# Splitting each weight tile with one instruction of 2048 columns on ACT and on DVE

## Chip, cores and metric

The kernel runs on one core of a Trainium2 chip. The metric is the device time of one execution in microseconds, as the median of several runs.

## What is computed

Two transformer blocks, one behind the other, on 256 tokens of width 2048, in float32. Cut to what matters:

```python
# first block
x = layer_norm(ALPHA * x + hybrid_mixer(x))           # sparse latent attention + block attention, gated, out1
x = layer_norm(ALPHA * x + mem_cross_attention(x, mem))
x = layer_norm(ALPHA * x + (silu(x @ w_g) * (x @ w_u)) @ w_down)        # up1, down1
# second block; shift, scale, gate = silu(c) @ w_ada + b_ada
x = x + gate1 * (concat(fourier_mix(u), mlstm_bidirectional(q, k, v, gates)) @ w_out)   # out2
x = x + gate2 * ((silu(conv(a)) * conv(v)) @ w_down)                    # up2, down2
return rms_norm(x)
```

Nearly all of the work is products of the 256 tokens with weight matrices of the first and the second block, 438 tiles of 1 MB.

## The kernel before

**Stream of weights.** The weights lie in memory as one stream of tiles, each 128 partitions by 2048 float32 columns (1 MB), in the order in which the stages use them (`TILES`, line 62): latent, q_idx, v_moba, w_uk, w_uv, qk, gate_a, gates, out1, the four of the memory attention, up1 (88 tiles), down1 (44), the mLSTM's, fourier, out2, up2 (88), down2 (44). SyncE loads tile g into `raw[g % 4]` (lines 388 to 396) once `lo_ready` tells that tile g − 4 has been split.

**Split.** TensorE multiplies in the type fp32r. For float32 accuracy every operand is split in a high part (rounded) and a low part (the rest), and each product is three: high by high, high by low, low by high. For a weight tile, ScalarE (ACT) makes the high part, `whi <- raw`, in `upper(g)` (line 499, the instruction is line 514), and VectorE (DVE) makes the low part, `wlo = raw - whi`, in `rest(g)` (line 920, instruction line 929). Both work by halves of 1024 columns. `whi` and `wlo` have four slots of 1024 columns each, two tiles' worth. ACT may overwrite a slot once TensorE (PE) has counted up `weights_used` for the half four before:

```python
if h >= 4:
    act.wait_ge(weights_used, at(h - 3, i, 2 * per))
```

DVE waits for `hi_ready` of the half, PE for `lo_ready` of the half. `at(n, i, per)` is the semaphore value n in the first round of a hardware loop and per more in each further one.

**Products.** `product` (line 1533) takes one half of a tile: in T form (line 1559) 24 matmuls of 256 columns, in N form (line 1563) of up to 512. In up1, up2 and most projections four tiles fill a chunk, a pair of PSUM banks, which ACT or DVE reads out when PE is through with it. `wide_tile` (line 1575) serves out1, o_mem, down1, out2 and down2: 24 matmuls of 512 columns a tile (line 1600) into all eight banks; it also waits for `slo_ready`, the low part of the activations, which DVE makes tile by tile (lines 1120, 1136) from the high part of ACT (line 686).

**Order of the work.** Every engine runs its own program, written out by hand. In up1, ACT runs eight calls of `upper` a loop turn, and behind the one with s = 3 it reads a finished chunk:

```python
if s == 3:
    act.wait_ge(weights_used, at(through(g0 + s), i, 16))
    act.wait_ge(pair_read[(c0 + 1) % 2], at(reads(c0 - 1), i, 1))
    act.activation(silu[:], pair(c0), ACT.Silu).then_inc(pair_read[c0 % 2], 1)
```

Before a Silu, a Sigmoid or an Exp the compiler puts an ACT_TABLE_LOAD, and another at the head of a loop for the copies behind it. DVE does, beside the splits, `modulation` (line 961), 96 steps of the product silu(c) @ w_ada on tiles of 2048 columns that GpSimd's queue loads: 8 in out1, 66 in up1, 22 in down1. In the turns of a wide stage (`later_turns`) DVE's order is, for s = 0 to 3, low part of the activations (line 1136), `rest`, and for s = 1 and 2 a `modulation`. The row sums of the normalizations (lines 1173 to 1225), the split of the memory activations (`mhi` line 718, `mlo` line 1232) and the read-outs (line 553 and others) stand between the calls at the ends of the stages.

Of the kernel before, what the change touches and what calls it, by code (L numbers as in the profile page):

```python
# [6 lines left out]
F32 = mybir.dt.float32  # L7
# [3 lines left out]
ALU = mybir.AluOpType  # L11
ACT = mybir.ActivationFunctionType
# [106 lines left out]
def at(first, i=None, per=0):  # L119

    return first if i is None else i * per + first


def two_blocks(nc, x, xt, memt, stream, w_ada, cols, rows, ln_g, ln_b, norm_f, c_row, gate_bias, dft, out, max_store, gate_store):
    with ExitStack() as ctx:  # L125
        def sem(name):
            return ctx.enter_context(nc.semaphore(name))
# [3 lines left out]
        def sb(name, shape, dt=F32, offset=None):  # L131

            here = place[0] if offset is None else offset
            if offset is None:
                size = int(np.prod(shape[1:])) * (2 if dt == BF16 else 4)
                place[0] += -(-size // 32) * 32
            return nc.alloc_sbuf_tensor_at(name, shape, dt, offset=here)


        raw = [sb(f"raw{s}", [P, D]) for s in range(4)]  # L140
        whi = sb("whi", [P, 4, 1024], F32R)
        wlo = sb("wlo", [P, 4, 1024], F32R)
# [127 lines left out]
        first_half_landed = sem("first_half_landed")  # L270
        raw_landed = [sem(f"raw_landed{s}") for s in range(4)]
        hi_ready = sem("hi_ready")
        lo_ready = sem("lo_ready")
        weights_used = sem("weights_used")
# [216 lines left out]
        def _(act):  # L491
# [10 lines left out]
            def upper(g, i=None, per=0):  # L502

                if g >= G:
                    return
                for half in range(2):
                    h = 2 * g + half
                    if g == 0 and half == 0:
                        act.wait_ge(first_half_landed, 16)
                    elif g == 0 or half == 0:  # L510
                        act.wait_ge(raw_landed[g % 4], at(16 * (g // 4 + 1), i, 4 * per))
                    if h >= 4:
                        act.wait_ge(weights_used, at(h - 3, i, 2 * per))
                    act.activation(whi[:, h % 4], raw[g % 4][:, 1024 * half:1024 * half + 1024], ACT.Copy)\  # L514
                       .then_inc(hi_ready, 1)

            def x_first_upper(b):

# [46 lines left out]
            for b in range(2):  # L565
                x_first_upper(b)
            upper(g0)
            for b in range(2, 4):
                x_first_upper(b)
            upper(g0 + 1)  # L570
            for b in range(4, 8):
                x_first_upper(b)
            upper(g0 + 2)
            upper(g0 + 3)
            act.wait_ge(pair_read[CH["latent"] % 2], reads(CH["latent"]))
# [17 lines left out]
            for n in range(8):  # L593
                g = AT["v_moba"] + n
# [10 lines left out]
            g = AT["w_uk"]  # L605
# [3 lines left out]
            g = AT["w_uv"]  # L609
# [4 lines left out]
            with act.Fori(0, 3) as i:  # L614
                for s in range(8):
                    upper(g0 + s + 1, i, 8)
                    if s % 4 == 3:
                        read_out(CH["qk"] + s // 4, g0 + s, qk[:, bass.ds(at(s - 3, i, 8), 4)].rearrange("p k t -> p (k t)"),
                                 i=i, per=8)
# [3 lines left out]
            with act.Fori(0, 2) as i:  # L623
                for q in range(4):
                    g = g0 + 2 * q
# [32 lines left out]
            with act.Fori(0, 2) as i:  # L658
                for unit in range(2):
                    g, c = g0 + 8 * unit, c0 + 3 * unit  # L660
# [258 lines left out]
        def _(dve):  # L919
            order = Order(dve, dve_order)  # L920

            def rest(g, i=None, per=0):

                if g >= G:
                    return
                for half in range(2):
                    h = 2 * g + half
                    dve.wait_ge(hi_ready, at(h + 1, i, 2 * per))
                    dve.tensor_tensor(wlo[:, h % 4], raw[g % 4][:, 1024 * half:1024 * half + 1024], whi[:, h % 4].bitcast(F32),  # L929
                                      ALU.subtract).then_inc(lo_ready, 1)  # L930

            def x_first_rest(b):

# [31 lines left out]
            for b in range(2):  # L965
                x_first_rest(b)
            rest(g0)
            for b in range(2, 4):
                x_first_rest(b)
            rest(g0 + 1)  # L970
            for b in range(4, 8):
                x_first_rest(b)
            rest(g0 + 2)
            rest(g0 + 3)
            dve.wait_ge(weights_used, through(g0 + 2))
# [104 lines left out]
            with dve.Fori(0, 2) as i:  # L1080
                order.enter(i, 24)
                for q in range(4):
                    g = g0 + 2 * q
# [64 lines left out]
            for unit in range(4):  # L1148
                g, c = AT["gates"] + 8 * unit, CH["gates"] + 3 * unit
# [268 lines left out]
            for n in range(4):  # L1418
                g = AT["lstm_o"] + 4 * n
# [569 lines left out]
```

## Time and profile before

| | before |
|---|---|
| median of 3 runs | 2600.51 us (2598.02 to 2602.15) |
| profiled execution, its own time | 2601.53 us |
| its span | 2599.9 us |
| granted TensorE clock, mean | 0.985 |
| busy: PE, DVE, ACT | 97%, 63%, 48% |
| DMA | 582.19 MB, mean 224 GB/s |
| chain that ended last, largest items | PE L1559 18%, PE L1600 12% |

The busy shares are sums over the whole span. Idle time in the groups of the profile is the time that an engine stood before an instruction, with what ended it ("<-"). In a timeline a row is one or several instructions in a row of the same kind: start, time, engine, line, and in brackets the idle time before and who ended it. Engine times of neighbouring instructions overlap by some hundredths of a microsecond.

### The profile page before, as it was taken

The numbers are of one execution on the slowest core, as the hardware profiler recorded it, in microseconds if no ns is written. First come the engines' busy times: TensorE is split into PE (matmuls) and PEld (weight loads), VectorE is DVE, ScalarE is ACT, GpSimd is POOL, SyncE is SP. The second block draws the span as 40 slices with busy tenths as digits, with TensorE's granted clock in tenths as the row PEclk, the third lists the DMA queues.
The fourth block names the chain that finished last, engine by engine and source line by source line (L and its number), as shares of the span: only waits on it lengthen the run. The fifth ranks groups of instructions, "written<-read, shape, count | busy, mean of one in ns | idle before, by whom it ended". The sixth has DMA issues, their size and how long they took to land. (4 is left out here: it accounts for less than half of the span.)

```text
span 2599.9 us, 45820 instructions
## 1 busy us (share of the span) xinstructions
PE 2511.7 (97%) x17960; PEld 2346.5 (90%) x17960; DVE 1641.5 (63%) x1908; ACT 1247.5 (48%) x1503; POOL 88.8 (3%) x143
## 2 busy tenths in 40 slices
PE   7999999999989999999999969999899999999997
PEld 7799999998979999999888868978799999998885
DVE  5564675457767777777777764555666666665555
ACT  4444564444544445454444454444555555554443
POOL 0000000000100000000000000000000000000000
PEclk9999999999999999999999989999899999999998
DMA  7455445569548898989877725435455555555552
GB/s 268 166 185 192 153 146 182 189 252 361 201 156 326 333 351 325 350 325 349 345 289 289 268 99 205 173 120 192 148 194 194 193 192 191 192 199 180 192 193 97
DMA packets 80968, 582.19 MB, mean 224 GB/s; under 512 B 9052, under 2 KB 9212, under 8 KB 10752
## 3 DMA queue, kind: packets, MB, share of 16 engines
q1 hardware_dynamic: 64224, 462.97, 48.5%
q0 software_dynamic: 14528, 104.63, 10.5%
q10 hardware_dynamic: 2144, 13.58, 1.4%
q8 instruction: 52, 0.85, 0.1%
q14 instruction: 20, 0.16, 0.0%
HBM read 579.02 MB, written 2.12 MB: 224 GB/s over the span
## 5 line engine op out<-in xcount | busy, mean ns | idle before, releaser
L929 DVE TENSOR_TENSOR wlo<-raw,whi 128x1024 fp32r<-128x1024 f32 x876 | 1056.9, 1223 | 753.4 <-ACT whi L514 750.0
L514 ACT ACTIVATE whi<-raw 128x1024 fp32r<-128x1024 f32 x876 | 918.3, 1061 | 1007.6 <-PE ps L1559 591.8
L1559 PE MATMUL ps<-xhi,whi 128*128 128x256 f32 x4176 | 1156.1, 277 | 10.7 <-DVE xlo L953 4.5
L1559 PE MATMUL ps<-xhi,wlo 128*128 128x256 f32 x4176 | 1151.6, 276 | 0.0
L1559 PE MATMUL ps<-xlo,whi 128*128 128x256 f32 x4176 | 1151.6, 276 | 0.0
L1559 PEld LDWEIGHTS ps<-xhi,whi 128*128 128x128 f32 x4176 | 786.5, 188 | 12.0 <-DVE xlo L953 4.3
L1559 PEld LDWEIGHTS ps<-xlo,whi 128*128 128x128 f32 x4176 | 786.6, 188 | 0.3
L1559 PEld LDWEIGHTS ps<-xhi,wlo 128*128 128x128 f32 x4176 | 786.2, 188 | 0.0
L961 DVE SCALAR_TENSOR_TENSOR ada<-ada,cb 128x2048 f32<-128x2048 f32 x96 | 219.4, 2286 | 11.3 <-DMA ada<-in_w_ada 11.1
L1600 PE MATMUL ps<-whi,dhi 128*128 128x512 f32 x704 | 217.7, 391 | 4.1 <-DVE conv L1470 4.1
L1600 PE MATMUL ps<-wlo,dhi 128*128 128x512 f32 x704 | 217.6, 390 | 0.0
L1600 PE MATMUL ps<-whi,dlo 128*128 128x512 f32 x704 | 217.6, 390 | 0.0
L1600 PEld LDWEIGHTS ps<-whi,dhi 128*128 128x128 f32 x704 | 132.5, 189 | 31.9 <-issue 4.5
L1600 PEld LDWEIGHTS ps<-whi,dlo 128*128 128x128 f32 x704 | 132.7, 188 | 27.8
L1600 PEld LDWEIGHTS ps<-wlo,dhi 128*128 128x128 f32 x704 | 132.7, 188 | 27.7
L1563 PE MATMUL ps<-whi,xhi 128*128 128x512 f32 (+1 forms) x224 | 88.4, 395 | 11.1 <-DVE wlo L929 10.2
L1600 PE MATMUL ps<-whi,shi 128*128 128x512 f32 x288 | 89.7, 393 | 2.9 <-DVE slo L1120 2.9
L1600 PE MATMUL ps<-whi,slo 128*128 128x512 f32 x288 | 89.3, 391 | 0.0
L1600 PE MATMUL ps<-wlo,shi 128*128 128x512 f32 x288 | 89.2, 391 | 0.0
L1563 PE MATMUL ps<-whi,xlo 128*128 128x512 f32 (+1 forms) x224 | 86.5, 386 | 0.0
L1563 PE MATMUL ps<-wlo,xhi 128*128 128x512 f32 (+1 forms) x224 | 86.4, 386 | 0.0
L1470 DVE SCALAR_TENSOR_TENSOR conv<-ps,col,conv 128x255 f32<-128x255 f32 x176 | 72.7, 475 | 18.5 <-ACT conv L880 18.5
(272 smaller groups left out, 1852.8 us busy)
## 6 DMA issues: line engine op xcount, KB each, us to landing
raw<-in_stream SPq DMA_DIRECT2D x437, 1024.0 KB, 4.8
ada<-in_w_ada POOLq DMA_DIRECT2D x96, 1024.0 KB, 6.4
gamma<-in_ln_g ACTq DMA_DIRECT2D x3, 1024.0 KB, 9.8
beta<-in_ln_b ACTq DMA_DIRECT2D x3, 1024.0 KB, 14.4
xT<-in_xt SPq DMA_DIRECT2D x4, 512.0 KB, 11.2
mem_part<-in_memt ACTq DMA_DIRECT2D x2, 1024.0 KB, 6.7
res<-in_x ACTq DMA_DIRECT2D x1, 2048.0 KB, 14.1
gate_row<-gate_store POOLq DMA_DIRECT2D x2, 1024.0 KB, 5.3
```

Of the source, the lines that this page charges most:

```text
L514: act.activation(whi[:, h % 4], raw[g % 4][:, 1024 * half:1024 * half + 1024], ACT.Copy)\
L929: dve.tensor_tensor(wlo[:, h % 4], raw[g % 4][:, 1024 * half:1024 * half + 1024], whi[:, h % 4].bitcast(F32), ALU.subtract).then_inc(lo_re ...
L961: dve.scalar_tensor_tensor(out=ada[slot][:], in0=ada[slot][:], scalar=1.0, in1=cb[:], op0=ALU.mult, op1=ALU.mult, accum_out=mod[:, bass.ds ...
L1470: ins = dve.scalar_tensor_tensor(out=conv[:, q, S * m + to:S * m + to + S - 1], in0=bank[:, S * m + fro:S * m + fro + S - 1], scalar=col[: ...
L1559: ins = pe.matmul(o, w[:, k, P * m:P * m + P], a(kt), start=begins and n == 0 and m % 2 == 0, stop=ends and n == 2, skip_group_check=True)
L1563: ins = pe.matmul(o, a(kt)[:, P * m:P * m + P], w[:, k, :], start=begins and n == 0, stop=ends and n == 2, skip_group_check=True)
L1600: ins = pe.matmul(ps[:, 4 * t + 2 * half + n], a[:, s, P * t:P * t + P], w[:, h % 4, 512 * n:512 * n + 512], start=first and a is hi and w ...
```

## The change

From tile 2 on, `upper` issues one ACT instruction over the whole tile and `rest` one DVE instruction. ACT waits until PE has counted up `weights_used` for both halves of tile g − 2 (2g − 2), DVE for `hi_ready` of both halves, and each adds 2 to its semaphore. Tiles 0 and 1 are split by halves as before. PE's program, SyncE's, the buffers and every other step are unchanged.

```diff
--- before.py
+++ after.py
@@ -503,16 +503,18 @@
 
                 if g >= G:
                     return
-                for half in range(2):
-                    h = 2 * g + half
-                    if g == 0 and half == 0:
-                        act.wait_ge(first_half_landed, 16)
-                    elif g == 0 or half == 0:
-                        act.wait_ge(raw_landed[g % 4], at(16 * (g // 4 + 1), i, 4 * per))
-                    if h >= 4:
-                        act.wait_ge(weights_used, at(h - 3, i, 2 * per))
-                    act.activation(whi[:, h % 4], raw[g % 4][:, 1024 * half:1024 * half + 1024], ACT.Copy)\
-                       .then_inc(hi_ready, 1)
+                if g < 2:
+                    for half in range(2):
+                        if g == 0 and half == 0:
+                            act.wait_ge(first_half_landed, 16)
+                        else:
+                            act.wait_ge(raw_landed[g], 16)
+                        act.activation(whi[:, 2 * g + half], raw[g][:, 1024 * half:1024 * half + 1024], ACT.Copy).then_inc(hi_ready, 1)
+                    return
+                act.wait_ge(raw_landed[g % 4], at(16 * (g // 4 + 1), i, 4 * per))
+                act.wait_ge(weights_used, at(2 * g - 2, i, 2 * per))
+                act.activation(whi[:, 2 * (g % 2):2 * (g % 2) + 2].rearrange("p h n -> p (h n)"), raw[g % 4][:], ACT.Copy)\
+                   .then_inc(hi_ready, 2)
 
             def x_first_upper(b):
 
@@ -923,11 +925,17 @@
 
                 if g >= G:
                     return
-                for half in range(2):
-                    h = 2 * g + half
-                    dve.wait_ge(hi_ready, at(h + 1, i, 2 * per))
-                    dve.tensor_tensor(wlo[:, h % 4], raw[g % 4][:, 1024 * half:1024 * half + 1024], whi[:, h % 4].bitcast(F32),
-                                      ALU.subtract).then_inc(lo_ready, 1)
+                if g < 2:
+                    for half in range(2):
+                        h = 2 * g + half
+                        dve.wait_ge(hi_ready, h + 1)
+                        dve.tensor_tensor(wlo[:, h], raw[g][:, 1024 * half:1024 * half + 1024], whi[:, h].bitcast(F32),
+                                          ALU.subtract).then_inc(lo_ready, 1)
+                    return
+                dve.wait_ge(hi_ready, at(2 * g + 2, i, 2 * per))
+                both = slice(2 * (g % 2), 2 * (g % 2) + 2)
+                dve.tensor_tensor(wlo[:, both].rearrange("p h n -> p (h n)"), raw[g % 4][:],
+                                  whi[:, both].rearrange("p h n -> p (h n)").bitcast(F32), ALU.subtract).then_inc(lo_ready, 2)
 
             def x_first_rest(b):
```

In the program after, lines of ACT behind this place stand 2 further down and those of DVE 8.

The change moves the first wait of a loop turn relative to the table load. ACT, head of the loop of up1, before (L514 is the split, ISA and REGISTER_ALU set and count the values waited for, L779 is the silu read-out):

```order
L773 ISA
L513 ISA [waits raw_landed2]
L514 ACT_TABLE_LOAD
L514 ACTIVATE whi<-raw_51 128x1024 [waits weights_used]
L513 REGISTER_ALU
L514 ACTIVATE whi<-raw_51 128x1024 [waits weights_used]
```

and after (L516 is the split):

```order
L775 ISA
L515 ISA [waits raw_landed2]
L516 ACT_TABLE_LOAD [waits weights_used]
L516 ACTIVATE whi<-raw_51 128x2048
L515 REGISTER_ALU [waits raw_landed3]
L516 ACTIVATE whi<-raw_52 128x2048 [waits weights_used]
```

The table load came before the wait for `weights_used`; now it carries that wait. The same pair of rows stands at the head of the loop of up2.

ACT around the silu read-out of up1, before:

```order
L513 REGISTER_ALU
L514 ACTIVATE whi<-raw_50 128x1024 [waits weights_used]
L777 REGISTER_ALU
L778 REGISTER_ALU [waits weights_used]
L779 ACT_TABLE_LOAD
L779 ACTIVATE silu<-ps 128x1024 [waits pair_read1]
L513 REGISTER_ALU [waits raw_landed2]
L514 ACTIVATE whi<-raw_51 128x1024 [waits weights_used] x2
L513 REGISTER_ALU [waits raw_landed3]
L514 ACTIVATE whi<-raw_52 128x1024 [waits weights_used]
```

and after:

```order
L516 ACTIVATE whi<-raw_50 128x2048 [waits weights_used]
L779 REGISTER_ALU
L780 REGISTER_ALU [waits weights_used]
L781 ACT_TABLE_LOAD
L781 ACTIVATE silu<-ps 128x1024 [waits pair_read1]
L516 ACTIVATE whi<-raw_51 128x2048 [waits weights_used,raw_landed2]
L515 REGISTER_ALU [waits raw_landed3]
L516 ACTIVATE whi<-raw_52 128x2048 [waits weights_used]
```

The read-out has kept its place between two tiles; behind it come two splits of a half before and one of a whole tile after.

DVE in a later turn of down1, tiles 2 and 3 of the turn, before (L1136 the low part of the activations, L929 the split, L961 `modulation`):

```order
L1136 TENSOR_TENSOR dlo_118<-hid,dhi 128x256
L928 REGISTER_ALU
L929 TENSOR_TENSOR wlo<-raw_52,whi 128x1024 [waits hi_ready]
L928 REGISTER_ALU
L929 TENSOR_TENSOR wlo<-raw_52,whi 128x1024 [waits hi_ready]
L960 ISA
L961 ISA [waits ada_landed0]
L961 SCALAR_TENSOR_TENSOR ada_98,mod<-ada_98,cb 128x2048
L1135 REGISTER_ALU
L1136 ISA [waits shi_ready]
L1136 TENSOR_TENSOR dlo_118<-hid,dhi 128x256
```

and after (lines 8 further down, the split L937):

```order
L1144 TENSOR_TENSOR dlo_118<-hid,dhi 128x256
L935 REGISTER_ALU
L937 TENSOR_TENSOR wlo<-raw_52,whi 128x2048 [waits hi_ready]
L968 ISA
L969 ISA [waits ada_landed0]
L969 SCALAR_TENSOR_TENSOR ada_98,mod<-ada_98,cb 128x2048
L1143 REGISTER_ALU
L1144 ISA [waits shi_ready]
L1144 TENSOR_TENSOR dlo_118<-hid,dhi 128x256
```

The modulation still stands between the split and the low part of the next tile's activations; the split ahead of it is one instruction of twice the width.

## Rows read from the trace of the kernel before

**Rows 1.** The page, sections 1 and 5 (busy us, mean ns, idle, releaser)

```profile
PE 2511.7 (97%) x17960; PEld 2346.5 (90%) x17960; DVE 1641.5 (63%) x1908; ACT 1247.5 (48%) x1503; POOL 88.8 (3%) x143
...
L929 DVE TENSOR_TENSOR wlo<-raw,whi 128x1024 fp32r<-128x1024 f32 x876 | 1056.9, 1223 | 753.4 <-ACT whi L514 750.0
L514 ACT ACTIVATE whi<-raw 128x1024 fp32r<-128x1024 f32 x876 | 918.3, 1061 | 1007.6 <-PE ps L1559 591.8
L1559 PE MATMUL ps<-xhi,whi 128*128 128x256 f32 x4176 | 1156.1, 277 | 10.7 <-DVE xlo L953 4.5
```

**Rows 2.** Windows: stretch, length, busy us, clock, DMA share (up1, down1, up2, down2)

```profile
780.00:1258.00 478.00, 478.00 (x4210) 477.62 (x4209) 364.66 (x325) 225.02 (x215) 34.90 (x66) 1.00 0.88 336
1262.00:1480.00 218.00, 218.00 (x963) 180.50 (x963) 153.26 (x158) 96.95 (x119) 10.56 (x20) 1.00 0.78 300
1862.00:2330.00 468.00, 468.00 (x4132) 468.00 (x4131) 287.06 (x351) 255.04 (x288) 0.00 (x0) 1.00 0.55 195
2345.00:2575.00 230.00, 230.00 (x1015) 190.41 (x1015) 115.41 (x124) 100.31 (x123) 0.00 (x0) 1.00 0.50 178
```

**Rows 3.** Waits of PE for the split: us, times, longest

```profile
PE ps L1563 <- DVE wlo L929: 10.2, 1, 10.2
...
PE ps L1559 <- DVE wlo L929: 2.9, 1, 2.9
```

**Rows 4.** Timeline in up2, one half on ACT and DVE

```profile
1899.29 1.06 ACT L514 ACTIVATE whi<-raw 128x1024 fp32r<-128x1024 f32 x1 [1.66 <-PE ps L1559]
...
1900.39 1.23 DVE L929 TENSOR_TENSOR wlo<-raw,whi 128x1024 fp32r<-128x1024 f32 x1 [1.49 <-ACT whi L514]
```

**Rows 5.** Groups by shape on ACT and DVE, the rows of 2048 columns

```profile
L701 ACT ACTIVATE ps<-res 128x2048 f32<-128x2048 f32 x6 | 11.3, 1881 | 29.4 <-DVE res L1225 22.9 <-DVE res L1193 6.5
L592 ACT ACTIVATE cb<-cb 128x2048 f32<-128x2048 f32 x1 | 1.9, 1922 | 0.0
...
L1225 DVE TENSOR_TENSOR res<-res,xn 128x2048 f32<-128x2048 f32 x4 | 9.2, 2292 | 0.1
```

**Rows 6.** Timeline at the start, the tile that PE waited for

```profile
45.63 3.90 ACT L514 ACTIVATE whi<-raw 128x1024 fp32r<-128x1024 f32 x4
46.72 4.63 DVE L929 TENSOR_TENSOR wlo<-raw,whi 128x1024 fp32r<-128x1024 f32 x4 [0.53 <-ACT whi L514]
...
48.00 0.58 PE L1559 MATMUL ps<-xhi,whi 128*128 128x256 f32 x1 [2.94 <-DVE wlo L929]
```

**Rows 7.** Timeline of DVE in down1, a modulation and the low part

```profile
1329.08 2.28 DVE L961 SCALAR_TENSOR_TENSOR ada<-ada,cb 128x2048 f32<-128x2048 f32 x1
...
1331.30 0.42 DVE L1136 TENSOR_TENSOR dlo<-hid,dhi 128x256 fp32r<-128x256 f32 x1
```

**Rows 8.** Timeline of ACT in up1, silu read-out and loop head

```profile
886.24 1.28 ACT L779 ACT_TABLE_LOAD   x1 [4.44 <-PE ps L1559]
...
888.46 2.94 ACT L514 ACTIVATE whi<-raw 128x1024 fp32r<-128x1024 f32 x3
...
903.59 1.28 ACT L514 ACT_TABLE_LOAD   x1
905.22 1.06 ACT L514 ACTIVATE whi<-raw 128x1024 fp32r<-128x1024 f32 x1 [0.35 <-PE ps L1559]
```

**Rows 9.** Timeline of ACT at a gate's read-out and at that of lq

```profile
470.80 1.57 ACT L654 ACTIVATE sig<-ps,col 128x256 f32<-128x256 f32 x4 [4.61 <-PE ps L1559]
...
1550.92 1.03 ACT L553 ACTIVATE lq<-ps 128x1024 f32<-128x1024 f32 x1 [4.38 <-PE ps L1559]
...
1553.81 3.89 ACT L514 ACTIVATE whi<-raw 128x1024 fp32r<-128x1024 f32 x4
```

**Rows 10.** Timeline at the memory split on DVE and the entry of up1

```profile
654.81 2.35 DVE L1232 TENSOR_TENSOR mlo<-mem_part,mhi 128x1024 fp32r<-128x1024 f32 x2
...
780.09 3.91 ACT L514 ACTIVATE whi<-raw 128x1024 fp32r<-128x1024 f32 x4
...
782.50 0.35 PE L1559 MATMUL ps<-xhi,whi 128*128 128x256 f32 x1
```

## Prediction

> **What bounds the kernel now.** I read the page first. PE is busy for 2511.7 us of the span, 97% of it, and DVE for 63% and ACT for 48%; the split of the weights is by far the largest item of both, 876 instructions of 1223 ns on DVE and 876 of 1061 ns on ACT [rows 1]. The last columns of these two rows matter as much: before its splits DVE stood idle for 753.4 us in all, waiting for ACT, and ACT for 1007.6 us, waiting for PE. So neither engine is short of time on average; ACT waits for slots that PE gives back. Then the windows by stage: in up1, down1, up2 and down2 the busy time of PE equals the window to the last digit [rows 2], so no stall hides there and every stall that the change makes in them is new time. Then the waits of PE: for `wlo` it waited twice in the whole program, 10.2 and 2.9 us, both in the first 50 us [rows 3]. The bound is PE, and the question is only whether the split of a tile still arrives in time.
>
> **What the change does to the slack.** Measure everything from the start S of a tile on PE. In the timeline an ACT split of a half runs 1.06 us after 1.66 us of waiting for PE, so a half comes every 2.72 us and a tile lasts 5.44 [rows 4]; its 48 matmuls then stand 0.113 us apart, while one lasts 277 ns [rows 1], so the last one of a tile ends about 0.17 us into the next tile. With the step of a semaphore behind it, a release comes about 0.2 us after S. A half needs 1.06 us on ACT and 1.22 us on DVE, with 0.04 us from one to the other (1899.29 plus 1.06, then 1900.39) [rows 4].
>
> Before, a half could be split as soon as the half two tiles earlier was read, and only one half had to be ready when its tile began: from release to need lay three halves, 8.16 us, for a chain of 2.4 us, some 5.8 us of slack. After, a tile is split when the whole tile two before it is read, which is 0.2 us after the start of the tile in between, and must be whole before its own first matmul at 5.44: 5.24 us. The new chain is one ACT copy of 2048 columns, one DVE subtraction of 2048 columns, and two hand-overs. Neither instruction is in this trace. Bounds for ACT: from above twice 1061, 2122 ns [rows 1]; from below 1881 ns, the nearest row of the same width being 1922 ns (`cb`, SBUF to SBUF) [rows 5]; I take 1.92. For DVE: from above twice 1223, 2446 ns; the row of the same kind and width, a TENSOR_TENSOR of 2048 columns from SBUF to SBUF, says 2292 [rows 5], and from below nothing excludes a few per cent less, say 2.2; I take 2.29. The hand-over to PE is 0.06 us: a half begun at 46.72 ends at 47.94 and PE starts at 48.00 [rows 6]; I take 0.07. Sum: 1.92 + 0.04 + 2.29 + 0.07 = 4.32 us, against 5.24. **A plain tile keeps 0.92 us of slack**, and costs nothing. What covers it is that both engines are free at the release. Any ACT or DVE work that stands in the chain after the release costs its own length less 0.92.
>
> The DVE rows here hold a gain too: 2446 ns of two become 2290 of one, 0.16 us a tile, 68 us of DVE's busy time over 438 tiles, and 0.2 us a tile on ACT. I cost it at nothing where the engine is idle anyway (753 and 1008 us of idle time stand before the splits). The Trainium skill, in "VectorE: DVE Perf Modes", section "The TRN2 errata — SBUF-src ops pay a fixed extra latency per instruction", says that one large tile pays that latency once and many small ones each time. By that rule alone the kernel would gain, or stay; that result is the first rival. Another rule of the skill speaks against the change ("Perfetto Trace Analysis", section "Optimizing Scalar/DVE Operations"): where ACT and DVE are not saturated but hold up other engines, breaking instructions up may let work finish sooner. The change does the reverse.
>
> **The places where work stands in the chain.**
> - *down1 and out1: `modulation` ahead of the low part.* On DVE the order is: split, `modulation` (L961), low part of the activations (L1136), next split; PE needs that low part for its next tile. Before, 1329.08 to 1331.30 for the modulation, 2.22 us, and the low part at once behind it [rows 7], hidden. After, the split ends later: 0.2 + 1.96 (ACT and hand-over) + 2.22 (DVE to the next start) + 2.22 + 0.42 + 0.07 = 7.09 after S, against 5.44: 1.65 us of stall. The turn's second modulation starts from the tile so delayed and finishes 0.1 us before PE has run that tile, so nothing. Ten later turns of down1: 16.5 us. Three of out1: 5.0. There the split of the memory activations (`mlo`, 2.35 us) stands in the same position once: 1.7.
> - *up1: the silu read-out.* ACT reads a finished chunk when PE is through with it, ahead of the split that the same moment releases: table load 1.28 and silu, from 886.24 to 888.46, so 2.22 us [rows 8]. 2.22 − 0.92 = 1.30, 11 turns: 14.3 us. The 66 modulations of up1 come behind the split and ahead of the next release's DVE turn: 4.25 + 2.22 after the release, and DVE's next split cannot begin before 5.44 + 1.96. Hidden. The transfers are those of before; up1 uses 0.88 of the DMA engines [rows 2], and a refill has four tiles' time.
> - *Loop heads of up1 and up2: a table load that now waits.* Before, the load of 1.28 us ran at 903.59, ahead of the wait, and was done 0.35 us early [rows 8]. In the order of after the table load itself carries the wait for `weights_used`, because the copy's first wait moved in front of it. So 1.28 + 0.02 lies in the chain: 0.38 us each. Ten turns of either loop not counting the first: 7.6 us.
> - *mLSTM.* After the `lq` read-out ACT does a table load and an exponential: 1550.92 to 1553.81, 2.89 us [rows 9], less 0.92: 1.97; `lk` the same; the `g_m` one and a plain read of N form some 1.5 together. 5.4 us.
> - *Gates.* Four sigmoid read-outs of 1.57 us [rows 9], of which the next instruction overlaps 0.13 (as 1.03 and 1.28 us of silu and load take 2.22 and not 2.31 [rows 8]): 0.52 each, and one table load ahead of a read: 3.4. Some eight plain read-outs of 0.98 us: 0.06 each, 0.5.
> - *Start.* The split of the tile that PE waited for at 48.00 now must be whole: 45.63 + 4.32 = 49.95, so 1.95 later [rows 6]; two like it in the latent tiles, 0.6 each, between nothing and 1.95: 3.2 in all.
> - *Stage changes.* k_mem: the split of its first tile ends 1.9 us later, and `mlo` at 654.81 [rows 10] with the row sums behind it; its second tile 0.9 more; q_mem 0.5: 3.3. Entry of up1: ACT begins at 780.09 [rows 10]; the tile is whole at 784.41, and PE began it at 782.50 [rows 10]: 1.9. Entry of up2, in the same way, 1.4. Together 6.6.
> - *up2, out2, down2:* no modulation there; the taps and the silu come behind the split. Nothing beyond the loop heads.
>
> Sum: 23.2 (wide stages) + 14.3 + 7.6 + 5.4 + 3.9 + 3.2 + 6.6 = 64.2 us. The profiled execution took 2601.53 us; 2601.5 + 64.2 = 2665.7. The median of the three runs is 1.0 us lower, so **2664.7 us**, 2.5% slower. Bounds: with ACT at 2.12 and DVE at 2.45 the slack falls to 0.56, and the 65 or so stalls cost 0.36 more each, 20 us; with ACT at 1.88 and the loads of the loop heads uncounted it is 10 us less, and if half of the small terms (start, stage changes, gates) are absorbed another 6.
>
> **Rivals.** A measurement of this kernel can tell about 0.2% (5.2 us) from no change.
> - *Faster: fewer instructions win.* Where both engines stand in PE's way, at the six hand-overs between stages, some two splits each lie in front of row work: 12 × 0.16 to 0.2 us, and 13.1 us of PE's waits for `wlo` as their ceiling. −3 us: about 2597.5. It decides if the slack of a whole tile were above 2.9 us, so that neither silu nor modulation reached PE; the chain of 4.32 us against 5.24 speaks against it. 0.02.
> - *No change: the buffers hide it.* Same condition, without a gain: 2600. The idle 753 and 1008 us speak for it as totals; they are spread over the tiles and, with whole-tile slots, cannot be saved up for a crowded turn. That the change doesn't do what it says would end here too; the order of after shows the wide instructions from tile 2 on. 0.03.
> - *The table loads do not wait.* If the load runs ahead of the semaphore as now, 7.6 us fall away: 2657. 0.15.
> - *Every tile stalls.* If the chain of a plain tile were over 5.24 us, some 380 plain tiles pay the excess: 0.1 us each is 38 us, and the crowded turns pay 0.92 more each, 60 us: 2760 and above. It needs 0.92 us that no row shows; rows 5 speak against it. 0.05.
> - *The forecast*, stalls in crowded turns alone: 0.75.
>
> Range: 2644 to 2686, the forecast's own bounds and the third rival; the rest, one in ten, lies outside. Faster 0.02, same 0.03, slower 0.95.
>
> **What would show it.** In the profile of after: ACT 436 wide splits near 1.92 us, DVE near 2.29. PE less than full in up1 and down1, full in down2 and in plain tiles. Waits of PE: for `wlo` about 11 times 1.3 us and 10 times 0.4 in up1, ten of 0.4 in up2; for `dlo` ten times 1.65 us in down1. Wrong would be: PE waits in plain tiles; a chain from release to ready tile much off 4.3 us; down1 stalls twice a turn, or not at all; table loads at the loop heads that end before the release.

## Result: 2690.1 us, 3.4% slower

| | before | after |
|---|---|---|
| median of 3 runs | 2600.51 us | 2690.12 us (2689.82 to 2690.15) |
| span of the profiled execution | 2599.9 us | 2688.5 us |
| granted TensorE clock, mean | 0.985 | 0.983 |

The ratio after to before is 1.0344, 95% interval 1.033 to 1.0358: 89.6 us more, where 64 were forecast. The time lies 4 us above the range.

The page of after; the rows answer to [rows 1]:

```profile
PE 2536.3 (94%) x17960; PEld 2354.3 (88%) x17960; DVE 1597.0 (59%) x1472; ACT 1172.3 (44%) x1067; POOL 91.5 (3%) x143
...
L937 DVE TENSOR_TENSOR wlo<-raw,whi 128x2048 fp32r<-128x2048 f32 x436 | 999.4, 2292 | 970.0 <-ACT whi L516 969.9
L516 ACT ACTIVATE whi<-raw 128x2048 fp32r<-128x2048 f32 x436 | 836.2, 1918 | 1128.6 <-PE ps L1567 641.0
L1567 PE MATMUL ps<-xhi,whi 128*128 128x256 f32 x4176 | 1162.4, 278 | 39.5 <-DVE wlo L937 31.6
```

The two instructions took what the forecast took for them, 2292 and 1918 ns (2.29 and 1.92 us). DVE and ACT are less busy than before, 59 and 44% against 63 and 48%, and idle longer ahead of the split, 970 and 1129 us. The kernel became slower while both engines got less to do. PE's own busy time rose by 24.6 us, which the forecast did not have: the first matmuls behind each stall come more slowly, and at a few stage changes the granted clock is lower (both below).

The windows of up1, down1, up2 and down2, as [rows 2]:

```profile
804.00:1305.00 501.00, 482.48 (x4184) 478.16 (x4183) 357.21 (x230) 207.35 (x124) 35.02 (x66) 1.00 0.84 318
1320.00:1550.00 230.00, 214.22 (x928) 174.35 (x927) 143.95 (x115) 84.30 (x77) 10.09 (x20) 0.99 0.72 268
1950.00:2419.00 469.00, 465.90 (x4087) 463.94 (x4086) 271.97 (x263) 239.31 (x201) 0.00 (x0) 1.00 0.53 189
2440.00:2664.00 224.00, 224.00 (x990) 185.55 (x989) 107.40 (x81) 90.66 (x81) 0.00 (x0) 1.00 0.49 178
```

PE is short of the window by 18.5 us in up1, 15.8 in down1 and 3.1 in up2; in down2, where DVE has no modulation, it is full. The waits of PE, as [rows 3] (us in all, times, longest):

```profile
PE ps L1567 <- DVE wlo L937: 33.6, 43, 4.9
PE ps L1532 <- DVE xn L1216: 27.2, 2, 16.9
PE ps L1608 <- DVE dlo L1144: 17.5, 10, 1.9
...
PE ps L1532 <- DVE res L1201: 9.5, 2, 9.1
PE ps L1608 <- DVE slo L1144: 6.7, 4, 1.7
...
PE ps L1571 <- DVE wlo L937: 2.2, 2, 1.6
```

In before the two waits for row work, `xn` and `res`, were 4.0 us shorter together:

```profile
PE ps L1524 <- DVE xn L1208: 24.4, 2, 15.6
...
PE ps L1524 <- DVE res L1193: 8.3, 2, 7.9
```

Nearly all stalls sit where the forecast put them. Laid side by side matmul by matmul (start times of the n-th matmul in either trace), the two traces show that PE falls behind in steps, and between the steps it loses nothing: 1.55 us in each of the 11 silu turns of up1, 0.62 at each loop head of up1 and 0.61 at those of up2, 2.02 in a later turn of down1, 1.95 in four places of out1, 0.72 at each of four gates, 0.27 at the plain read-outs of qk. The forecast had no term for three of the steps: 1.26, 1.26 and 1.49 us at the ends of the memory attention, down1 and out2. There DVE's row work stands behind a split, now one of 2048 columns that ends later; at the end of the memory attention that split runs from 781.27 to 783.56 and the row work starts at 783.48 without a gap, while in before DVE had stood idle for 0.40 us, waiting for PE. By stage, in us:

| stage | forecast | measured |
|---|---|---|
| start to gates | 7.1 | 9.1 |
| attention, out1 | 6.7 | 8.6 |
| memory | 3.3 | 6.0 |
| up1 | 20.0 | 27.0 |
| down1 | 16.5 | 22.0 |
| mLSTM, out2 | 5.4 | 8.2 |
| up2 | 5.2 | 7.6 |
| down2 | 0 | 0.1 |
| sum | 64.2 | 88.6 |

**One silu turn, step by step.** Timeline of after in up1, ACT, then DVE and PE:

```profile
917.93 1.28 ACT L781 ACT_TABLE_LOAD   x1 [3.51 <-PE ps L1567]
919.22 1.03 ACT L781 ACTIVATE silu<-ps 128x1024 f32<-128x1024 f32 x1
920.15 1.91 ACT L516 ACTIVATE whi<-raw 128x2048 fp32r<-128x2048 f32 x1
```

```profile
922.16 2.29 DVE L937 TENSOR_TENSOR wlo<-raw,whi 128x2048 fp32r<-128x2048 f32 x1 [5.35 <-ACT whi L516]
...
924.51 0.39 PE L1567 MATMUL ps<-xhi,whi 128*128 128x256 f32 x1 [1.24 <-DVE wlo L937]
924.73 0.28 PE L1567 MATMUL ps<-xlo,whi 128*128 128x256 f32 x1
924.85 0.28 PE L1567 MATMUL ps<-xhi,wlo 128*128 128x256 f32 x1
```

PE began the tile in between at 917.67 (48 matmuls of 0.113 us before its last). ACT starts at 917.93, 0.26 us later, not 0.20. Silu moves the split by 2.22 us, as forecast. From the end of the split, 920.15 + 1.91 = 922.06, DVE needs 0.10 us to start, not 0.04. It ends at 924.45, and PE starts 0.06 later. That is 6.84 us after 917.67, so PE is 1.40 us late (a tile lasts 5.44); its first matmul then lasts 0.39 us and the second starts 0.22 behind it in place of 0.11, another 0.11, and the ten behind them lose 0.04 more. Together 1.55, against 1.30.

**The loop head** of up1, ACT in after:

```profile
941.23 1.28 ACT L516 ACT_TABLE_LOAD   x1 [3.50 <-PE ps L1567]
942.52 1.93 ACT L516 ACTIVATE whi<-raw 128x2048 fp32r<-128x2048 f32 x1
```

ACT stands idle for 3.50 us until PE releases the slot, and only then runs the table load; in before the load was over by then [rows 8].

**A turn of down1**, DVE, then PE:

```profile
1385.51 2.29 DVE L937 TENSOR_TENSOR wlo<-raw,whi 128x2048 fp32r<-128x2048 f32 x1 [2.90 <-ACT whi L516]
1387.72 2.29 DVE L969 SCALAR_TENSOR_TENSOR ada<-ada,cb 128x2048 f32<-128x2048 f32 x1
...
1389.93 0.42 DVE L1144 TENSOR_TENSOR dlo<-hid,dhi 128x256 fp32r<-128x256 f32 x1
```

```profile
1390.48 0.73 PE L1608 MATMUL ps<-whi,dhi 128*128 128x512 f32 x2 [1.74 <-DVE dlo L1144]
```

The split, the modulation and the low part follow one another without a gap, and PE waits for the low part. The second modulation of the turn costs nothing, as forecast: ten waits for `dlo`, not twenty.

### The profile page after: what moved, and what is told of

Read it like the earlier page. It is cut to its first block and busy times, and to the rows that moved or that the text cites. A ratio compares the mean times of both kernels' runs of the same rounds, so it can differ in the third digit from the quotient of the medians.

```text
span 2688.5 us, 45101 instructions
## 1 busy us (share of the span) xinstructions
PE 2536.3 (94%) x17960; PEld 2354.3 (88%) x17960; DVE 1597.0 (59%) x1472; ACT 1172.3 (44%) x1067; POOL 91.5 (3%) x143
## 5 line engine op out<-in xcount | busy, mean ns | idle before, releaser
L937 DVE TENSOR_TENSOR wlo<-raw,whi 128x2048 fp32r<-128x2048 f32 x436 | 999.4, 2292 | 970.0 <-ACT whi L516 969.9
L516 ACT ACTIVATE whi<-raw 128x2048 fp32r<-128x2048 f32 x436 | 836.2, 1918 | 1128.6 <-PE ps L1567 641.0
L1608 PE MATMUL ps<-whi,dhi 128*128 128x512 f32 x704 | 219.7, 393 | 21.6 <-DVE dlo L1144 17.5
L1571 PE MATMUL ps<-whi,xhi 128*128 128x512 f32 (+1 forms) x224 | 88.5, 395 | 13.3 <-DVE wlo L932 10.3
L440 POOL DMA_DIRECT2D ada<-in_w_ada x94 | 49.9, 531 | 829.7 <-DVE ada L969 829.7
```

The source lines that it names most:

```text
L440: pool.dma_start(ada[s % 2][:], w_ada[at(n0 + s, i, per)]).then_inc(ada_landed[s % 2], 16)
L516: act.activation(whi[:, 2 * (g % 2):2 * (g % 2) + 2].rearrange("p h n -> p (h n)"), raw[g % 4][:], ACT.Copy)\
L937: dve.tensor_tensor(wlo[:, both].rearrange("p h n -> p (h n)"), raw[g % 4][:], whi[:, both].rearrange("p h n -> p (h n)").bitcast(F32), AL ...
L1571: ins = pe.matmul(o, a(kt)[:, P * m:P * m + P], w[:, k, :], start=begins and n == 0, stop=ends and n == 2, skip_group_check=True)
L1608: ins = pe.matmul(ps[:, 4 * t + 2 * half + n], a[:, s, P * t:P * t + P], w[:, h % 4, 512 * n:512 * n + 512], start=first and a is hi and w ...
```

## Experiments

Theory W says that an instruction of 2048 columns lengthens the chain from a release to a tile that PE can start, and whatever ACT or DVE does ahead of it in that chain comes out as a stall. Theory R, the rival, says that the coarser release of the slots is the cost, whatever the width. A ratio and a difference to before are against the runs of before on the same chip; "less than after" is the difference of the medians, and after was timed in one set of runs only. The medians of before in the four sets lie within 1.1 us.

### Which half of the change costs

Two halves an engine, released by whole tiles:

```diff
 act.wait_ge(weights_used, at(2 * g - 2, i, 2 * per))
-act.activation(whi[:, 2 * (g % 2):2 * (g % 2) + 2].rearrange("p h n -> p (h n)"), raw[g % 4][:], ACT.Copy)\
-   .then_inc(hi_ready, 2)
+for half in range(2):
+    act.activation(whi[:, 2 * (g % 2) + half], raw[g % 4][:, 1024 * half:1024 * half + 1024], ACT.Copy)\
+       .then_inc(hi_ready, 1)
...
-dve.wait_ge(hi_ready, at(2 * g + 2, i, 2 * per))
-dve.tensor_tensor(wlo[:, both].rearrange("p h n -> p (h n)"), raw[g % 4][:],
...
+for half in range(2):
+    slot = 2 * (g % 2) + half
+    dve.wait_ge(hi_ready, at(2 * g + half + 1, i, 2 * per))
+    dve.tensor_tensor(wlo[:, slot], raw[g % 4][:, 1024 * half:1024 * half + 1024], whi[:, slot].bitcast(F32),
+                      ALU.subtract).then_inc(lo_ready, 1)
```

> From after, one thing undone: from tile 2 on, ACT and DVE again issue two instructions of 1024 columns a tile, but the slots stay released by whole tiles (both halves wait for tile g-2). Theory W (the cost is the length that an instruction of 2048 columns adds to the chain from release to a tile that PE can start): a first half is ready 0.20 + 1.06 + 0.03 + 1.22 + 0.06 = 2.57 us after the tile before it began, so 2.9 us of slack; the silu turns (2.22), the loop heads and the gates cost nothing; in down1 DVE has both halves behind it at 3.67, the modulation at 5.9 and the low part at 6.4, against 5.44: about 1.0 us in each of 10 turns, the same in out1; some 3 at k_mem. In all 12 to 20 us over before: about 2617 us. Theory R (the release by whole tiles is what costs, whatever the width): 70 to 90 us over before, as after, with waits of PE for wlo in the silu turns of up1.

Measured 2618.9 us, ratio 1.0071 (1.0054 to 1.0088), span 2617.0. Waits of PE for the low part, and the only one for the split in a T form, which before had too:

```profile
PE ps L1610 <- DVE dlo L1146: 7.3, 10, 0.7
...
PE ps L1610 <- DVE slo L1146: 3.2, 4, 0.8
PE ps L1569 <- DVE wlo L939: 2.9, 1, 2.9
```

Of the 89 us, the release by whole tiles alone makes 18, most of it in down1 and out1, where PE waits 0.7 us and loses 1.02 us in all a turn, and nothing in the loop of up1. So theory R falls as the main cause, but a fifth of the cost is its own: with the wide instructions taken back, the coarser release still costs.

The width on one engine only. ACT whole, DVE by halves, both behind `hi_ready` of the tile:

```diff
 dve.wait_ge(hi_ready, at(2 * g + 2, i, 2 * per))
-dve.tensor_tensor(wlo[:, both].rearrange("p h n -> p (h n)"), raw[g % 4][:],
...
+for half in range(2):
+    dve.tensor_tensor(wlo[:, slot], raw[g % 4][:, 1024 * half:1024 * half + 1024], whi[:, slot].bitcast(F32),
+                      ALU.subtract).then_inc(lo_ready, 1)
```

> From after, DVE alone by halves again: ACT splits a whole tile with one instruction, DVE waits for it and issues two of 1024 columns, each counted up by itself; release by whole tiles. Theory W: first half ready 0.26 + 1.91 + 0.10 + 1.22 + 0.06 = 3.55 us after the start of the tile before, slack 1.9. Silu turns 2.22 - 1.9 + 0.11 (restart of PE) = 0.44, eleven times 5 us; lq and lk 1.1 each; loop heads, gates and plain reads nothing; down1 and out1 as in after, 2.0 a turn, because the modulation stands behind both halves: 28 us; k_mem and the start some 5. In all about 40 us over before: 2641 us. Theory R: as after, 2690. On the hand-over from ACT to DVE, which grew from 0.03 us in before to 0.10 in after: if it goes with the width of the instruction that waits it is 0.03 here, if with the width of the one that is waited for, 0.10.

ACT by halves with release by halves, DVE whole:

```diff
-act.wait_ge(weights_used, at(2 * g - 2, i, 2 * per))
...
+for half in range(2):
+    act.wait_ge(weights_used, at(2 * g + half - 3, i, 2 * per))
+    act.activation(whi[:, 2 * (g % 2) + half], raw[g % 4][:, 1024 * half:1024 * half + 1024], ACT.Copy)\
+       .then_inc(hi_ready, 1)
```

> From after, ACT alone by halves again, each half released by itself as in before; DVE waits for both and subtracts the whole tile with one instruction. Theory W: the second half decides: 0.20 + 1.06 + 0.10 + 2.29 + 0.06 = 3.71 us, slack 1.7, where ACT could do the first half early; where a read-out stands ahead of both halves it cannot, and the silu turn costs 2.22 + 1.99 + ... as much as in after, 1.5 us each, 17 us; lstm 7 us, gates 3; the loop heads nothing; down1 about 1.0 a turn, 10, and out1 4; start, k_mem and entries some 10. In all 50 to 55 us over before: 2652 us. Theory R says that with the release by halves back, nearly all is back: under 15 us over before. Hand-over from ACT to DVE: 0.10 if it goes with the width of the one that waits, 0.03 if with the one that is waited for.

Measured 2648.4 us (ratio 1.018, 1.0163 to 1.0197) and 2661.1 us (1.0232, 1.0215 to 1.0249), 47 and 60 us over before, somewhat more than expected of either. The waits of PE of the first, then of the second:

```profile
PE ps L1609 <- DVE dlo L1145: 17.5, 10, 1.9
...
PE ps L1609 <- DVE slo L1145: 6.7, 4, 1.7
PE ps L1568 <- DVE wlo L938: 5.3, 4, 3.8
```

```profile
PE ps L1568 <- DVE wlo L938: 29.5, 24, 5.0
...
PE ps L1609 <- DVE dlo L1145: 7.3, 10, 0.7
```

They trade places. With DVE by halves the silu turns almost vanish (5.3 us of `wlo` against 33.6; a silu turn costs PE 0.4 us), since PE begins on the first half, while down1 keeps its 17.5, since the modulation stands behind both halves. With ACT by halves `wlo` stays near after's (29.5), since the read-out stands ahead of both halves (24 times in place of 43: the table load of the loop heads is ahead of the wait again and costs nothing there), and down1 falls to 7.3. That release by halves is back in the second and helps little, 60 us of 89 stay, speaks against R once more.

### Are the stalls the pieces of work that the forecast named?

Each was moved out of the chain by itself. The modulation, in the later turns of the wide stages:

```diff
 dve.tensor_tensor(lo[:, s], ...).then_inc(slo_ready, 1)
+if ada0 is not None and s in (2, 3):
+    modulation(ada0 + 2 * n0 + s - 2, i, 2)
 rest(g0 + s + 1, i, 4)
-if ada0 is not None and s in (1, 2):
-    modulation(ada0 + 2 * n0 + s - 1, i, 2)
```

> After with one step moved: in the later turns of down1 and out1 the modulation stands behind the low part of the next tile's activations (s = 2 and 3, ahead of the split) instead of ahead of it. If the stall of 2.00 us in each of 10 turns of down1 and of 1.95 in 3 of the 4 stalls of out1 is the modulation ahead of the low part, all of these go, since DVE is through with low part and modulation at 7.1 us after the start of the tile before, and the next high part comes at 7.7: 26 us less than after, about 2664 us. If DVE simply has too much to do in a turn (rival), the next split starts late and the stall comes back as a wait for wlo: within 5 us of after.

Measured 2663.8 us (ratio 1.0243, 1.0226 to 1.026): 26.3 less than after. No wait for `dlo` is left, PE passes the later turns of down1 at the pace of before, and the wait for `wlo` stays, 34.1 us against 33.6; the rival that DVE has too much to do falls.

The silu read-out of up1, behind the split, waiting for the same tile:

```diff
-if s == 3:
-    act.wait_ge(weights_used, at(through(g0 + s), i, 16))
+if s == 4:
+    act.wait_ge(weights_used, at(through(g0 + 3), i, 16))
```

> After with one step moved: in up1 the silu read-out (table load and silu) stands behind the split that the same release frees, not ahead of it. Theory W: the 11 stalls of 1.51 us go, since the split starts at the release and the 2.2 us of silu end before the next one: 16.6 us less than after, 2673.5 us. Rival (the load on ACT decides, not the order): ACT does as much as before in a turn, so the stalls stay, within 4 us of after.

Measured 2672.3 us (ratio 1.0275, 1.0258 to 1.0293): 17.8 less than after. The wait for `wlo` went from 33.6 us in 43 times to

```profile
PE ps L1567 <- DVE wlo L937: 20.4, 33, 4.9
```

Matmul by matmul, the 11 steps of 1.55 us are gone and the ten of 0.61 at the loop heads stay.

The table load. The first version added one instruction of one column at the loop heads and a small tile, placed behind `wlo`, for it to write (4 bytes a partition, for which the kernel's placement of tiles takes 32):

```diff
 wlo = sb("wlo", [P, 4, 1024], F32R)
+scratch = sb("scratch", [P, 1])
...
 with act.Fori(0, FC) as i:
+    act.activation(scratch[:], col[:, 0:1], ACT.Copy)
```

> After with one ACT instruction of one column added at the head of the loops of up1 and up2, ahead of the split and its wait, so that the table load comes before it and no longer carries the wait for weights_used. Theory: the stalls of 0.60 us at the loop heads, 10 in up1 and 10 in up2, are this load in the chain; they go, 12 us less than after: 2678 us. If they are something else at the loop head (the branch, the counting of the semaphore values), they stay: 2690 us.

Measured 2744.4 us (ratio 1.055, 1.0532 to 1.0567), 54 us more than after. The waits for `wlo` did fall, to 24.3 us in 24 times; but in 100 us of up2 PE, busy throughout, began 845 matmuls where in before it began 885. Two more kernels have the same added tile, and so the same burden, and tell nothing of their own edits:

> After with all three: modulation behind the low part, silu behind the split, table load first. If the parts add up: 26.5 + 16.6 + 12 = 55 us less than after, 2635 us, which leaves 34 us over before: start, gates, memory, mLSTM, the entries of the stages. If the engines are short of time once the order is right, less of it comes back.

> The three together, and every tile outside a hardware loop split by halves with release by halves as in before; only tiles in loops (most of up1, down1, up2, down2, qk) have instructions of 2048 columns. Theory W: what is left is the entry of up1, where the first loop turn still begins with a wide ACT instruction (0.9 us and a slower clock behind it, 1 to 2 us), and four read-outs in qk of 0.25: about 4 us over before, 2605 us. If wide instructions gain anything where they don't stall, it shows here: less than before. If some stall comes from elsewhere, it stays in the stage where after has it.

They measured 2706.1 (ratio 1.0403, 1.0371 to 1.0435; four runs between 2695 and 2711) and 2688.8 us (1.034, 1.0323 to 1.0357). Whether the place of the tiles does it was tried on the kernel before:

```diff
 wlo = sb("wlo", [P, 4, 1024], F32R)
+gap = sb("gap", [P, 1])
```

> The kernel before with nothing but an unused tile of 32 bytes behind wlo, so that all tiles behind it lie 32 bytes further on. In the first try of the table load, 100 us of up2 held 845 matmuls where before had 885, with PE busy throughout. If the place of the tiles does that, before gets as slow without any other change: 45 to 60 us more, about 2650 us. If it needs the wide instructions, it stays at 2601 us.

Measured 2684.0 us (ratio 1.029, 1.0244 to 1.0336; three of the four runs within 1.3 us, one 23 us lower). The window 2200 to 2300 us in up2 of this kernel, then of before:

```profile
2200.00:2300.00 100.00, 100.00 (x845) 100.00 (x844) 58.00 (x70) 53.54 (x61) 0.00 (x0) 1.00 0.52 187
```

```profile
2200.00:2300.00 100.00, 100.00 (x885) 100.00 (x884) 62.26 (x79) 54.72 (x63) 0.00 (x0) 1.00 0.53 189
```

32 bytes of place, and nothing else, make PE start 845 matmuls in the time of 885, 4.7% more time for each. Stage by stage the matmuls of 256 columns take 4.7% more time, in up1 as in up2, and those of 512 columns in down1 and down2 2.9%. The cost, 84 us, is more than the 45 to 60 expected. With the tiles back in their places, the added instruction writing an unused column of a tile that was there, `misc(47)`:

```diff
 with act.Fori(0, FC) as i:
+    act.activation(misc(47), col[:, 0:1], ACT.Copy)
```

> The table load first again, but with no tile moved: the one-column instruction writes an unused column of a tile that is there already. The first try had added a tile of 32 bytes behind wlo, and the places of all tiles behind it had moved; there the loop heads were back to no stall, while matmuls came more slowly in all stages, so it could not price the load. Theory: 12 us less than after, 2678 us. If the 54 us over after of the first try came from the added instruction itself, they are here too: 2744 us.

Measured 2676.8 us (ratio 1.0294, 1.0277 to 1.0311): 13.3 less than after. Timeline of ACT, a loop head of up1:

```profile
935.80 1.28 ACT L776 ACT_TABLE_LOAD   x1
937.10 0.20 ACT L776 ACTIVATE small<-col 128x1 f32<-128x1 f32 x1
939.29 1.93 ACT L516 ACTIVATE whi<-raw 128x2048 fp32r<-128x2048 f32 x1 [2.00 <-PE ps L1569]
```

The load is over at 937.08 and the small copy at 937.30, 2.0 us before PE releases the slot, and in the loop of up2 PE keeps the pace of before. So it was the load in the chain.

### Do the parts add up, and what is left?

The three edits in one kernel:

> Modulation behind the low part, silu behind the split, table load first, with no tile moved. If the parts add up: 2690 - 26 - 18 - 12 = 2634 us, 33 us over before, in start, gates, memory, mLSTM and the entries of the stages. If the engines are short of time once the order is right, less comes back.

Measured 2635.3 us (ratio 1.0129, 1.0112 to 1.0146): 54.9 less than after; the parts by themselves gave 26.3 + 17.8 + 13.3 = 57.4. The 2.5 us between them are not assigned. In its windows of up1 and down1 PE is full again:

```profile
804.00:1285.00 481.00, 481.00 (x4202) 479.84 (x4202) 361.35 (x235) 210.21 (x134) 34.88 (x66) 1.00 0.88 339
1300.00:1515.00 215.00, 215.00 (x951) 178.07 (x950) 147.17 (x119) 88.47 (x79) 10.30 (x20) 1.00 0.76 284
```

Then the same with every tile outside a hardware loop by halves, on both engines, released by halves:

```diff
-if g < 2:
+if i is None:
     for half in range(2):
...
+        if g >= 2:
+            act.wait_ge(weights_used, 2 * g + half - 3)
```

> The three together, tiles outside hardware loops by halves with release by halves, and no tile moved. Left over before: the entry of up1 (0.9 us, a slower clock behind it for 1 to 2), the read-outs in qk, 0.25 each: about 4 us over before, 2605 us. If wide instructions gain anything where they don't stall it shows as less than before: 2598 us or lower.

Measured 2606.7 us (ratio 1.0026, 1.0015 to 1.0037), 6.5 over before, where 4 were expected. One wait for `wlo` is left that before does not have, 1.9 us, at the entry of up1, and the wait for `xn` is as long as in after, 2.7 us over before's:

```profile
PE ps L1536 <- DVE xn L1220: 27.1, 2, 16.8
```

That is row work behind a wide split at the ends of down1 and out2, which the expectation, like the forecast, left out. Where the wide instructions stall nothing they also gain nothing. A stretch of up2, of this kernel, then of before:

```profile
1884.00:2330.00 446.00, 446.00 (x3938) 446.00 (x3937) 266.65 (x264) 233.99 (x209) 0.00 (x0) 1.00 0.54 193
```

```profile
1884.00:2330.00 446.00, 446.00 (x3938) 446.00 (x3937) 275.09 (x338) 243.30 (x275) 0.00 (x0) 1.00 0.55 193
```

DVE and ACT are 8 and 9 us less busy, and PE begins the same 3938 matmuls. No version here beats the kernel before.

## Why the prediction was wrong in size

- *What bounds the kernel; the chain from release to ready tile; where work stands in it.* Right but for the three ends of stages below. Plain tiles cost nothing, the crowded turns pay, each in the place named, and taking away the three named pieces took away 54.9 us. The mechanism held, and sizes failed.
- *The durations, 1.92 and 2.29 us, and the pieces ahead (2.22 for silu, 2.22 for the modulation, 1.28 for the load).* Right to 0.01 us.
- *"A plain tile keeps 0.92 us of slack ... costs its own length less 0.92."* This is the step that failed: the slack was sized too large. Its hand-overs were taken from instructions of 1024 columns. Measured: ACT starts 0.26 us after the start of the tile, not 0.20, and DVE 0.10 after ACT, not 0.04. That leaves 0.81. (The 0.26 could have been read in before: a table load that waits starts that late there too.) And a stall costs PE 0.15 us more than its length, since the matmuls behind it start late. Effective slack 0.67: 2.22 − 0.67 gives the 1.55 of the silu turns, 1.29 − 0.67 the 0.62 of the loop heads. In the down1 turn release and start of PE were later still (0.35 and 0.13 us): 2.02 against 1.65. Over some 70 stalls 0.2 to 0.37 us each is about 16 us of the 24 that were missing.
- *The clock* was in no term. At the entry of up1 the forecast had 1.9 us of stall; the stall was 2.0, but behind it PE ran in part at the lower of its two clock levels, 1.2 GHz. Two stretches behind it in after (clock in the third column from the right):

```profile
808.20:811.60 3.40, 3.40 (x19) 3.40 (x20) 3.40 (x3) 0.16 (x1) 0.58 (x1) 0.62 0.63 217
811.60:815.00 3.40, 3.40 (x28) 3.40 (x28) 3.14 (x3) 0.00 (x0) 0.00 (x0) 0.88 0.90 342
```

  19 matmuls in 3.4 us, where a start every 0.113 us makes 30. Against before PE lost 1.6 us there beside the stall, and about as much again in one place at k_mem and in one at the first later turn of down1 (clock 0.50 from 1341.5 to 1344.9), about 5 us in all. What PE had done before differs: at k_mem it had waited 1.7 us for a low part and 3.7 for row work, at the entry of up1 for row work and 1.8 us for the split, in down1 1.9 us for a low part. The nine like stalls of down1, and the silu and loop-head stalls, brought no lower clock. Nor does the same stall always bring it: in the run with silu behind the split PE waits as long at the entry of up1, 1.8 us, and the clock behind it is full:

```profile
810.00:813.40 3.40, 3.40 (x32) 3.40 (x32) 3.40 (x3) 0.00 (x0) 0.58 (x1) 1.00 0.81 284
```

  What decides it is open. The mean granted clock of 0.985 over 2599.9 us and 0.983 over 2688.5 puts the time lost to it at 39 and 46 us, about 7 us more, part of it while PE waited anyway.
- *The ends of the memory attention, down1 and out2* were in no term: 1.26, 1.26 and 1.49 us, 4.0 together, as the waits for `xn` and `res` show. Some 0.5 of it comes back directly behind. With the 16 and the 5 this accounts for the 24 us that were missing.
- *The range* reached up by 20 us for slower instructions, which did not come, and held nothing for hand-overs, clock and stage ends. By its own figures it was short too: 65 stalls of 0.36 us are 23.4, not 20. Even that bound, 2688, lies below the measured time.
- *Rivals.* Every-tile stalls did not come: down2 is full. The table loads did wait. Fewer instructions won nothing: DVE's busy time fell by 44 us and ACT's by 75, and the time rose. That a single large instruction pays a fixed part once is what the Trainium skill says ("VectorE: DVE Perf Modes", section "The TRN2 errata — SBUF-src ops pay a fixed extra latency per instruction"). The rows bear it out, 2292 ns against twice 1223. The other rule of the Trainium skill is to break instructions up where the engines are not saturated but hold up others ("Perfetto Trace Analysis", section "Optimizing Scalar/DVE Operations"). That is the one that the time followed, 2600.5 to 2690.1 us.

## What to carry to other kernels

Where one engine feeds another through two slots, compare the length of the chain from release to ready with the time that one slot lasts, and count everything that stands in the chain in the crowded turns; idle percentages say nothing of it. Larger instructions saved busy time on the feeding engines here and cost the consumer latency; whether they pay where the feeder is saturated no run here shows. Once a stall exists, price it by start-to-start times of the consumer, with its restart and its clock, take hand-over times from instructions as wide as the new ones, and look at the row work behind the last tile of each stage as well.

## Not expected of the hardware

- **An instruction of 2048 columns that waits for a semaphore starts 0.06 to 0.07 us later than one of 1024.** Between ACT and DVE it goes with the one that waits. ACT whole, DVE by halves: ACT ends at 2204.10 and DVE starts 0.03 later. ACT by halves, DVE whole: ACT ends at 2203.78 and DVE starts 0.10 later. Timelines of either in up2, ACT and DVE:

```profile
2202.18 1.92 ACT L516 ACTIVATE whi<-raw 128x2048 fp32r<-128x2048 f32 x1 [1.13 <-PE ps L1568]
...
2204.13 2.36 DVE L938 TENSOR_TENSOR wlo<-raw,whi 128x1024 fp32r<-128x1024 f32 x2 [3.07 <-ACT whi L516]
```

```profile
2202.72 1.06 ACT L517 ACTIVATE whi<-raw 128x1024 fp32r<-128x1024 f32 x1 [1.61 <-PE ps L1568]
...
2203.88 2.29 DVE L938 TENSOR_TENSOR wlo<-raw,whi 128x2048 fp32r<-128x2048 f32 x1 [1.58 <-ACT whi L517]
```

  The median is 0.03 over the 512 hand-overs of before in which DVE waited and 0.10 over the 399 of after. On ACT, in up1, a copy of 1024 columns starts 0.20 us after the start of the tile or half in before, one of 2048 columns 0.26 in after. But the table load, which has no columns, also starts after 0.26, in before as in after, so the width alone is not the rule. Whether the width does it for the copies, or the form of the access, was not tried apart.
- **Tiles 32 bytes further on in SBUF slowed the matmuls of 256 columns by 4.7% and those of 512 by 2.9%**, and the kernel before by 84 us. Which of the moved tiles matters was not tried.
- **A semaphore wait can land on the table load.** Whether it did depended on the waits ahead of the first copy of the loop: with two copies of 1024 columns behind one wait the load came first, with one copy of 2048 it carried the wait, 0.62 us a turn.
